# Another order for the input projections of a two-layer encoder: the A values in front of the transposes, the compressed K and V turned behind the A heads' Q and K

## The reference, cut to what matters

```python
for l in range(DEPTH):                       # DEPTH = 2, 512 tokens, D_MODEL = 1024
    mod = c_act @ w_ada[l] + b_ada[l]        # 1024 -> 6144
    sh_a, sc_a, g_a, sh_m, sc_m, g_m = split(mod, 6)
    h = x * (1 + sc_a) + sh_a
    a_q, a_k, a_v, b_cq, b_ckv, b_kr, c_q, c_k, c_v = split(h @ w_in[l])
    # widths:  256, 256, 256,  384,   256,   32,  512, 128, 128
    y_a = dilated_mixture(a_q, a_k, a_v, rel_bias)
    y_b = mla_attention(b_cq, b_ckv, b_kr, ...)   # rms_norm(b_cq) @ w_uq, rms_norm(b_ckv) @ w_ukv, rope on b_kr
    y_c = axial_gqa(c_q, c_k, c_v, ...)           # rms_norm and 2-D rope on q and k
    y = concat(y_a, y_b, y_c) @ w_o[l]
    x = layer_norm(ALPHA * x + (1 + g_a) * y, ...)
    h = x * (1 + sc_m) + sh_m
    x = layer_norm(ALPHA * x + (1 + g_m) * (relu(h @ w1[l]) ** 2 @ w2[l]), ...)
```

## Time and profile before

| | us |
|---|---|
| median of 3 runs | 1403.76 (1403.68 to 1404.70) |
| the profiled execution's own time | 1406.55 |
| its span | 1404.7 |
| PE busy in it | 1315.9 (94%) |
| DVE busy | 989.6 (70%) |
| ACT busy | 606.0 (43%) |
| POOL busy | 332.1 (24%) |

### The profile page before, as it was taken

How to read it: one execution, slowest core, us unless ns; L and a number is a source line. 1 busy time by engine, 2 the same in 40 slices (tenths; PEclk the granted TensorE clock), 3 DMA queues, 4 the chain that set the end, 5 groups by cost and what they waited for, 6 DMA issues and landing times.

```text
span 1404.7 us, 19902 instructions
## 1 busy us (share of the span) xinstructions
PE 1315.9 (94%) x6888; PEld 1118.5 (80%) x6888; DVE 989.6 (70%) x1676; ACT 606.0 (43%) x1260; POOL 332.1 (24%) x427
## 2 busy tenths in 40 slices
PE   4998989899999999999999899889999999999995
PEld 2888777788988888888879878678788888888884
DVE  6668789975688665755775887999377954545577
ACT  0446479871632223222254546789253222222321
POOL 0013056650324000000030404967040700000005
PEclk9999999999999999999999998999999999999998
DMA  8864500003344443442246462000225433333322
GB/s 289 301 205 147 191 27 1 28 3 111 103 151 154 155 153 95 157 156 91 83 120 235 135 217 86 1 28 1 90 68 180 154 94 98 98 97 96 98 93 95
DMA packets 88165, 164.54 MB, mean 117 GB/s; under 512 B 8024, under 2 KB 18648, under 8 KB 88080
## 3 DMA queue, kind: packets, MB, share of 16 engines
q1 hardware_dynamic: 87408, 161.08, 35.2%
q10 hardware_dynamic: 672, 2.36, 0.5%
HBM read 159.21 MB, written 4.19 MB: 116 GB/s over the span
## 4 chain that ended last, share of the span: by engine, by line
PE 65%; DVE 13%; DMA 7%; ACT 6%; POOL 4%; issue 3%; SPq 0%; POOLq 0%; ACTq 0%; DVEq 0%
PE bank L1505 21%; PE bank L1506 20%; PE bank L1507 20%; DMA slab_raw<-in_w_in 5%; DVE ada_sum L938 2%; PE bank L1722 2%; DVE pt_lo L1178 2%; DMA ada_w<-in_w_ada 1%; DVE smax L1165 1%; ACT slab_hi L606 1%; PE bank L1536 1%; POOL prob L536 1%; DVE q_hi L1146 1%; DVE stats L1218 1%; ACT pt_hi L822 1%
## 5 line engine op out<-in xcount | busy, mean ns | idle before, releaser
L1505 PE MATMUL bank<-hT_hi,slab_hi 128*128 128x512 f32 (+1 forms) x640 | 235.9, 369 | 2.4 <-ACT kB L755 2.4
L1506 PE MATMUL bank<-hT_lo,slab_hi 128*128 128x512 f32 (+1 forms) x640 | 235.4, 368 | 0.0
L1507 PE MATMUL bank<-hT_hi,slab_lo 128*128 128x512 f32 (+1 forms) x640 | 235.4, 368 | 0.0
L1280 DVE TENSOR_TENSOR slab_lo<-slab_raw,slab_hi 128x512 fp32r<-128x512 f32 x240 | 172.3, 769 | 66.9 <-ACT slab_hi L880 44.3
L1505 PE MATMUL bank<-slab_hi,h_hi 128*128 128x512 f32 x512 | 201.5, 394 | 0.3 <-DVE slab_lo L1280 0.3
L1507 PE MATMUL bank<-slab_hi,h_lo 128*128 128x512 f32 x512 | 199.3, 389 | 0.0
L1506 PE MATMUL bank<-slab_lo,h_hi 128*128 128x512 f32 x512 | 199.3, 389 | 0.0
L1505 PE MATMUL bank<-slab_hi,hT_hi 128*128 128x384 f32 (+3 forms) x448 | 153.8, 343 | 10.5 <-DVE slab_lo L982 4.0
L982 DVE TENSOR_TENSOR slab_lo<-slab_raw,slab_hi 128x512 fp32r<-128x512 f32 (+3 forms) x144 | 83.2, 586 | 106.2 <-ACT slab_hi L606 106.0
L498 POOL TENSOR_SCALAR mv<-mv 128x1 f32<-128x1 f32 x16 | 5.5, 345 | 642.3 <-DVE mv L1226 641.6
L1506 PE MATMUL bank<-slab_lo,hT_hi 128*128 128x384 f32 (+3 forms) x448 | 151.2, 338 | 0.0
(11 more groups left out here) (199 smaller groups left out, 2565.2 us busy)
## 6 DMA issues: line engine op xcount, KB each, us to landing
slab_raw<-in_w SPq DMA_DIRECT2D x256, 256.0 KB, 2.7
ada_w<-in_w_ada SPq DMA_DIRECT2D x48, 1024.0 KB, 6.1
slab_raw<-in_w_in SPq DMA_DIRECT2D x48, 192.0 KB, 5.1
slab_raw<-in_w_o SPq DMA_DIRECT2D x32, 256.0 KB, 2.7
slab_raw<-in_w_in SPq DMA_DIRECT2D x16, 256.0 KB, 4.2
band<-bias_rows SPq DMA_DIRECT2D x8, 448.0 KB, 3.2
slab_raw<-in_w_in SPq DMA_DIRECT2D x16, 144.0 KB, 4.7
X<-in_x SPq DMA_DIRECT2D x1, 2048.0 KB, 9.6
```

The costliest lines, as they stand in the source:

```text
L1280: dve.tensor_tensor(slab_lo[:, slot, :], slab_raw[:, slot, :], f32(slab_hi[:, slot, :]), ALU.subtract).then_inc(slab_lo_done, 1)
L1505: pe.matmul(dst, a_hi, w_hi, start=first, stop=False)
L1506: pe.matmul(dst, a_hi, w_lo, start=False, stop=False)
L1507: return pe.matmul(dst, a_lo, w_hi, start=False, stop=last)
```

## The change

On PE, `av` and `ad0` move from behind `tk` to in front of `tc`; `aqk` follows `tk`, and `tkv` moves from in front of `ad0` and `aqk` to behind them. With their new places the jobs get other banks: `av`, `tc`, `aqk`, `uq` have the upper four, `ad0`, `tk`, `tkv`, `uk` the lower four. Where PE waited for a whole job's banks (`free_after`) before `tk`, `aqk`, `uq` and `bv`, it now waits bank by bank.

On ACT, `vA` and the gate stand directly behind split 43, in front of `qC`, `kC` and `cqT_hi`; the squares and the scaling of `ckv` stand ahead of that; `ckvT_hi` and `kB` stand behind `qkA`. Splits 44 to 47 are spread around `cqT_hi`, and splits 54 and 55 stand behind `qB`. On DVE, two of the four `qC` banks are read out by `tensor_copy`; `cqT_lo` and `ckvT_lo` move back. The rope key gets a tile of its own (`krope`), so that ACT reads a `bckv` bank in two instructions. SP's program is unchanged, and so are DVE's rope tiles and splits 24 to 39 with their `ada` steps.

```diff
-        ("tc", 4, 0), ("tk", 1, 3), ("av", 4, 0), ("tkv", 1, 2), ("ad0", 2, 0), ("aqk", 4, 0),
-        ("uq", 2, 2), ("uk", 2, 0), ("bv", 4, 0), ("ad1", 2, 0), ("ad2", 2, 0),
+        ("av", 4, 0), ("ad0", 2, 0), ("tc", 2, 2), ("tk", 1, 3), ("aqk", 4, 0), ("tkv", 1, 2), ("uq", 2, 2),
+        ("uk", 2, 0), ("bv", 4, 0), ("ad1", 2, 0), ("ad2", 2, 0),
...
@@ ACT @@
                 slab_job_done(B_CKV)
                 for t in range(TT):
-                    evac(ckv[:, t, :], banks(JOB["bckv"])[t][:, 0:RKV + ROPE])
-                for b in range(4):
+                    src = banks(JOB["bckv"])[t]
+                    act.activation(ckv[:, t, :], src[:, 0:RKV], ACT.Copy)
+                    evac(krope[:, t, :], src[:, RKV:RKV + ROPE])
...
+                for k in range(4):
+                    split(40 + k, 512)
+
+                slab_job_done(A_V)
+                for t in range(TT):
+                    evac(vA[:, t, :], banks(JOB["av"])[t][:, 0:256])
+                ada_evac("ad0", 0)
+                for b in range(2):
                     act.wait_ge(bank_ready, l * B_LAYER + ready_before("tc") + b + 1)
                     evac(qC[:, b, :], banks(JOB["tc"])[b][:, :])
                 act.wait_ge(bank_ready, l * B_LAYER + ready_before("tk") + 1)
                 evac(kC[:, :], banks(JOB["tk"])[0][:, :])
+                split(44, 512)
...
@@ DVE @@
+                for k in range(4):
+                    split(40 + k, 512)
+                    ada(3, k)
+                for b in range(2, 4):
+                    dve.wait_ge(bank_ready, l * B_LAYER + ready_before("tc") + b + 1)
+                    dve.tensor_copy(qC[:, b, :], banks(JOB["tc"])[b][:, :]).then_inc(evac_dve, 1)
+                split(44, 512)
...
-                for k in range(8):
+                for b in range(2):
+                    dve.wait_ge(bT_hi_done, l * 5 + 3 + b + 1)
...
+                for k in range(6, 8):
                     split(48 + k, 512)
...
@@ PE @@
                 chunk_job("bckv", B_CKV, 288)
+                chunk_job("av", A_V, 256)
+                ada_job("ad0", 0)
                 free_after("tc")
...
-                free_after("tk")
                 for b in range(4):
+                    if b < 2:
+                        pe.wait_ge(evac_act, l * A_LAYER + a_before("ad0") + b + 1)
...
-                chunk_job("av", A_V, 256)
+                for k in range(8):
+                    slab_ready(l * SLABS + 8 * A_QK + k + 1)
+                    for c in range(4):
+                        if k == 0 and c < 2:
+                            pe.wait_ge(evac_act, l * A_LAYER + a_before("tc") + c + 1)
+                        elif k == 0:
+                            pe.wait_ge(evac_dve, l * D_LAYER + d_before("tc") + c - 1)
+                        ins = three(banks(JOB["aqk"])[c][:, :], slab_hi[:, k, c * P:(c + 1) * P],
+                                    slab_lo[:, k, c * P:(c + 1) * P], hT_hi[:, k, :], hT_lo[:, k, :], k == 0, k == 7)
+                    ins.then_inc(slab_free, 1)
                 free_after("tkv")
...
-                ada_job("ad0", 0)
-                chunk_job("aqk", A_QK, 512)
-
-                free_after("uq")
...
                 for c in range(4):
+                    pe.wait_ge(evac_act, l * A_LAYER + a_before("aqk") + c + 1)
...
-                free_after("bv")
                 for t in range(TT):
+                    if t < 2:
+                        pe.wait_ge(evac_act, l * A_LAYER + a_before("uq") + t + 1)
+                    else:
+                        pe.wait_ge(evac_dve, l * D_LAYER + d_before("uq") + t - 1)
```

More of the change, by code:

```diff
@@ L199, in trunk @@
         bands = [nc.alloc_sbuf_tensor_at(f"band{i}", [P, 896], F32, offset=ada_at + 8192 * i) for i in range(2)]
-        ckv = over("ckv", [P, TT, 288], 0)
+        ckv = over("ckv", [P, TT, RKV], 38912)
+        krope = over("krope", [P, TT, ROPE], 92160)
         cst = over("cst", [P, TT, 640], 18432)
@@ L721, in _ @@
                 for t in range(TT):
-                    evac(ckv[:, t, :], banks(JOB["bckv"])[t][:, 0:RKV + ROPE])
-                for b in range(4):
+                    src = banks(JOB["bckv"])[t]
+                    act.activation(ckv[:, t, :], src[:, 0:RKV], ACT.Copy)
+                    evac(krope[:, t, :], src[:, RKV:RKV + ROPE])
+                act.wait_ge(evac_act, l * A_LAYER + a_before("av"))
+                for t in range(TT):
+                    act.activation(sq_ckv[:, t, :], ckv[:, t, :], ACT.Square, scale=RKV ** -0.5,
+                                   accum_out=msq[:, t, 11:12]).then_inc(bms_done, 1)
+                for k in range(6, 8):
+                    split(32 + k, 256)
+                for t in range(TT):
+                    act.wait_ge(brstd_done, l * 8 + 4 + t + 1)
+                    act.activation(ckv[:, t, :], ckv[:, t, :], ACT.Copy, scale=rms[:, t, 11:12]
+                                   ).then_inc(ckv_scaled, 1)
+                for k in range(4):
+                    split(40 + k, 512)
+                slab_job_done(A_V)
+                for t in range(TT):
+                    evac(vA[:, t, :], banks(JOB["av"])[t][:, 0:256])
+                ada_evac("ad0", 0)
+                for b in range(2):
                     act.wait_ge(bank_ready, l * B_LAYER + ready_before("tc") + b + 1)
@@ L731, in _ @@
                                    scale=colpack[:, 32 + b:33 + b]).then_inc(bT_hi_done, 1)
[L732 to L738, removed]
-                    split(40 + k, 512)
[L740 to L748, removed]
+                for k in range(5, 8):
+                    split(40 + k, 512)
+                for k in range(6):
+                    split(48 + k, 512)
+                slab_job_done(A_QK)
+                for b in range(4):
+                    evac(qkA[:, b, :], banks(JOB["aqk"])[b][:, :], scale=SC_A if b < 2 else 1.0)
                 for b in range(2):
@@ L756, in _ @@
                 ins.then_inc(evac_act, 1)
[L757 to L766, removed]
                 for b in range(2):
@@ L1079, in _ @@
                 dve.wait_ge(evac_act, l * A_LAYER + a_before("bckv") + 4)
-                kr = ckv[:, :, RKV:]
+                kr = krope[:, :, :]
                 t1 = rt1[:, 0:128].rearrange("p (t j) -> p t j", t=TT)
@@ L1096, in _ @@
                                              op0=ALU.mult, op1=ALU.subtract).then_inc(evac_dve, 1)
-                for k in range(4):
+                for k in range(5, 8):
                     split(40 + k, 512)
+                for k in range(4, 8):
                     ada(3, k)
+                dve.wait_ge(up_hi_done, l * 5 + 5)
+                for j in range(5):
+                    dve.tensor_tensor(u_lo[:, j, :], u_raw[:, j, :], f32(u_hi[:, j, :]), ALU.subtract
+                                      ).then_inc(up_lo_done, 1)
+                for k in range(6):
+                    split(48 + k, 512)
+                    for n in (2 * k, 2 * k + 1):
+                        ada(4 + n // 8, n % 8)
                 for b in range(2):
@@ L1655, in _ @@
                         w = P if b < 2 else ROPE
-                        ins = pe.transpose(banks(JOB["tkv"])[b][0:w, t * P:(t + 1) * P],
-                                           ckv[:, t, b * P:b * P + w], ident[:, :])
+                        src = ckv[:, t, b * P:b * P + P] if b < 2 else krope[:, t, :]
+                        ins = pe.transpose(banks(JOB["tkv"])[b][0:w, t * P:(t + 1) * P], src, ident[:, :])
                     ins.then_inc(bank_ready, 1)
-                ada_job("ad0", 0)
-                chunk_job("aqk", A_QK, 512)
-                free_after("uq")
                 pe.wait_ge(up_hi_done, l * 5 + 5)
                 pe.wait_ge(up_lo_done, l * 5 + 5)
+                pe.wait_ge(evac_dve, l * D_LAYER + d_before("tk") + 3)
                 for c in range(4):
+                    pe.wait_ge(evac_act, l * A_LAYER + a_before("aqk") + c + 1)
                     for k in range(3):
-                        if c == 0 and k == 0:
-                            pe.wait_ge(evac_dve, l * D_LAYER + d_before("tk") + 3)
                         ins = three(banks(JOB["uq"])[c][:, :], u_hi[:, k, c * P:(c + 1) * P],
```

## The result

The changed kernel takes 1410.3 us (median of 5 runs, 1410.04 to 1414.37), against 1403.76 before: a ratio of 1.0036, 95% interval 1.0021 to 1.0052. It is slower by some 5 us (by the ratio) to 6.5 us (by the medians); the forecast was 1410.8 and slower by 7.0. The profiled execution itself took 1414.37 us with a span of 1412.6; that of before had 1406.55 and 1404.7.

A forecast was written before the change was run, and what follows sets the result against it. Prediction: PE, in flight 94% of the span, is bound before aqk by a chain of waits through slab 43. Layer 0: 2.6 + 1.4 - 0.3 = 3.7; layer 1: 3.3; together 7.0 on 1403.76 gives 1410.8 us, range 1405.5 to 1415.0.

The forecast's parts named there:

- Start of av: PE's gap behind bckv: av waits for the same DVE work as tc did, so the 4.7 us gap stays; gain 0.
- Cost of av: PE before slab 43 lands: av ends at 136.3, ad0 at 138.3; 5.4 us of gained slack and no time.
- Slab 43: Load in front of vA: lands 0.3 us earlier, bounds 1.0 us earlier and 0.5 later.
- 32 transposes: PE between vA and aqk: they take 6.1 and 5.7 us, so aqk starts 2.6 and 2.2 us later.
- Evacuations: Bank read-outs by ACT and DVE before aqk: bank-by-bank waits cost 0, or 0.7 us if their cover were gone.
- tkv: Its 12 transposes come behind aqk on PE, where nothing hides them: cost 1.4 us in each layer.
- bv: Single-bank waits shrink the start-to-start distance at bv: -0.3 us per layer.
- Tail: DVE's qB sums behind late split 54 end at about 186.5, k_lo due at about 186.8: just covered, cost 0.
- After the tail: From the start of attention, 3 to 4 us later, to layer 1: nothing changed.
- The clock rule: Skill's rule that transposes neither keep nor bring up PE's clock; prediction said the trace disagrees; every transpose would cost 0.21 us.
- rival (b): Clock down through the transposes and 4 us of aqk at half clock: 12.6 us slower, 1416.4; chance 0.05.
- Rival (c): Clock stays up in the short stop before tc: transposes cost 3.8 us, total +2.8, 1406.6; chance 0.12.

The follow-up runs named there:

- e1: Changed kernel with ACT's split 43 moved behind the read-out of vA and the gate: 1400.14 us, ratio 0.9959 to the kernel before.
- e2: Changed kernel with DVE's rope tiles 2 and 3 moved behind the splits of slabs 38 and 39: 1403.46 us, ratio 0.9984 to before.
- e3: Changed kernel with the two products of ad0 done twice, same result: 1405.91 us, ratio 1.0000 to the kernel before.
- e8: The changed kernel as it is, run again in a later series: 1411.25 us, ratio 1.0036 to the kernel before.
- e5: Changed kernel with the edits of e1 and e2 together: 1392.42 us, ratio 0.9899 to the kernel before; repeated in another series, 1394.77 us, 0.9924.
- e7: Changed kernel with each of the twelve transposes of tkv done twice, same result: 1412.37 us, ratio 1.0045 to the kernel before.
- e10: e5 with DVE's two qC copies behind ada(3, 1) instead of ada(3, 3): 1395.40 us, ratio 0.9930 to the kernel before.
- e4: Changed kernel with single-bank waits before tk, aqk, uq and bv turned back into whole-job waits: 1413.69 us, ratio 1.0056 to before.

## Why the prediction was right, step by step

The mechanism was right: the gap is not filled, slab 43 still decides when `vA` is read, and 32 transposes and `tkv` come onto the path. How near the total came is in part luck, as the last step shows.

*Start of av: gain 0.* Right. The gap stayed over 5 us and DVE's `slab_lo` ended it, in both layers. *Cost of av.* It ended at 135.81 where 136.3 was said, and the gate at 137.7 where 138.3 was; all of it lay within the wait for slab 43. (The 5.4 us of slack has no sum in the text: by its own rows `av` gained 2.7 us and the gate 5.6. Nothing rests on it.)

*Slab 43, 0.3 us earlier.* The chain was right in each link, and e1 and e2 move it from both its ends. The size was 0.7 us in layer 0 (split at 138.81, 22.8 us behind the end of `bckv`; before, at 140.1, 23.5) and 0.2 in layer 1, inside the bounds of 1.0 and -0.5 that the prediction set. Read off the two profiles directly it is 1.3 us in layer 0, a little outside the 1 us given as a sign; but the whole stretch began 0.56 us sooner there. Load 7's slab took 5.33 and 6.42 us against 6.38 and 6.67, although slabs 44 to 46 share with it.

*32 transposes, 6.1 and 5.7 us.* 5.13 and 5.75. In layer 0 the clock came back after 3.4 us of work, in layer 1 about as before. With slab 43 that gives `aqk` 1.14 and 2.36 us later, where 2.6 and 2.2 were said. So this sign failed in layer 0: `aqk` started at 145.72 us, not at 147 to 148. The floor of 3.8 us was too high: 3.42 to 3.47 us at full clock in e1, e3 and e8.

*Evacuations: 0.* Right. PE waited for no bank in `tk` or `aqk`; DVE's `tensor_copy` of a bank takes 0.69 us, ACT's copies of the rope key about 0.2 each. The 0.7 us "if that cover were gone" turned up in e5 as 0.91: there `aqk` starts sooner and the copies stand behind split 43.

*tkv, 1.4 us.* 1.23 between its start and `uq` in layer 0, 1.3 by e7; 1.58 in layer 1, with the late `qkA` told under e10. *bv, -0.3 us.* -0.24 and -0.07: right in layer 0, hardly there in layer 1.

*Tail, 0.* Right that DVE's sums stay covered, by a hair. DVE's timeline of the changed kernel:

```profile
181.49 2.78 DVE L1135 TENSOR_TENSOR qB<-tmp 32x512 f32<-32x512 f32 x4
184.63 1.40 DVE L1151 TENSOR_TENSOR k_lo<-kC,k_hi 64x512 fp32r<-64x512 f32 x2 [0.36 <-ACT k_hi L796]
```

0.36 us of idle is left of the 2.2, where 0.3 was said. But the term missed something else: `bv` to the scores took 0.6 and 0.5 us more. The 32 one-column matmuls L1489 ran 4.49 us instead of the 3.63 that the trace of before has, with a granted clock of 0.77 in that window against 0.95, and the scores waited 0.26 us for ACT behind them. It is not a fixed part of the change: from `bv` to the scores e1 and e2 have 6.94 to 6.99 us, e8 8.08 and 7.22. *After the tail.* "Nothing changed from there to layer 1" did not hold in the profile (1.85 us more). The granted clock was 0.83 in 185 to 215 us, against 0.95 before, and 0.94 in 245 to 275, against 1.00. In the profile of e8 that stretch is 605.06 us, 0.6 more than before.

So the sum of 7.0 us stands on errors that cancel: transposes and slab 43 in layer 0 were put 1.5 us too dear, and a tail of 1.1 us was not seen. That the stages of the first profile add up to 7.1 is luck to this extent. The profile of e8, counted the same way against the same profile of before, gives 5.2 us, and the ratios of both series say 5.0; in e8 the clock held in layer 0. The changed kernel is some 5 us slower, and 7.0 was on the high side, by about one loss of the clock.

*The clock rule.* The windows of e3 show 31 transposes at 1.00 throughout, and in the change the clock came back in the middle of transposes. The Trainium skill (TensorE: Matmul & The Clock Gate, Part 4: PE-mode transpose), by which they neither keep nor bring up the clock, is not borne out by this kernel's fp32 transposes; rival (b) did not happen. Rival (c) did not happen in the profile, did in one layer of e8, and could be had at will by e3.

## What to carry to other kernels

When a product is moved into a gap, ask what ends the gap for the moved product as well, and then who reads its result and what stands in front of that reader in its engine's program: here a split that nothing needed yet, waiting for a late slab, kept the finished A values waiting for 3.6 and 5.0 us. A reordering may be slower by itself and still be what makes the real gains possible: two small edits on top of the new order made the kernel 11 to 14 us faster than before; in the old order one of them gave 1.8 us and the nearest form of the other cost 13. Remove both waits of a chain before judging either, and expect the next one (slab 53) close behind.

## What the runs showed of the hardware that was not expected

PE's clock after a stop is not decided by the stop's length alone: 2.4 us, and it fell (e4, layer 0); 2.9 us, and it fell (first profile, layer 0); 3.7 us, and it held (e8, layer 0). Filling 1.7 us of it with useless products held it in both layers of e3's profile and made the kernel 5.0 us faster, 3.9 of it in the transposes.

Around the 32 matmuls of one column, some 0.11 us each, the clock falls although PE is busy nearly all the time. In each of the 13 kept profiles, in both layers, it is 1.00 in their first 2 us and 0.50 to 0.80 in the first 2 us of the scores behind them. Only the moment differs: within them in the changed kernel (0.77 in 4.6 us), behind them in layer 0 of e1 (1.00 in 178.4 to 182.2 us). That the narrow matmuls are the reason was not tested.
